# Hybrid attention layer on eight cores: 440 of the 128x128 transposes are issued as DMA transposes from SBUF to SBUF

## The chip, the cores and the metric

The kernel runs on all 8 cores of one Trainium2 chip. Each core computes one batch element of 4096 rows; the cores exchange nothing. The metric is the device time of the slowest core in microseconds (us).

## The reference

One decoder layer with two parallel branches, cut to what is computed:

```python
h = rms_norm(x, g_pre)
qa, ka, va, za, qb, kb, vb, zb, lr, gate_a, gate_b = split(h @ w_in)
# branch A: causal attention with two maps per head, ALiBi bias, 4 heads
p = softmax(qa @ ka.T * scale + bias)
oa = rms_norm((p[:, :, 0] - lam * p[:, :, 1]) @ va, g_sub_a) * (1.0 - lam_init)
ya = (oa * silu(za)) @ w_up_a
# branch B: gated linear attention (GLA) in chunks, 4 heads
glog = log_sigmoid(lr @ w_alpha + b_alpha) / 16
ob = rms_norm(gla_chunked(qb, kb, vb, glog), g_sub_b)
yb = (ob * silu(zb)) @ w_up_b
# merge
y = sigmoid(gate_a) * ya + sigmoid(gate_b) * yb
return x + rms_norm(y @ w_out, g_post)
```

## The kernel before

The 4096 rows are cut into 8 tiles of 512 rows (`t`), and a tile into 4 pieces of 128 rows (`s`). Stage `t` runs the attention of tile `t` (4 heads `h`, key blocks `kb` two at a time). Between the attention steps it runs a list of small units of matmuls, in this order: the merge and output of tile `t-1` (`u_e`, `u_f`, with the gate `u_za` of tile `t` ahead of the merge), the GLA projections of tile `t` (`gproj`: low rank, `vb`, `zb`, then `QB`/`KB`), and the Q, K, V projections of tile `t+1` (`u_qkv`) merged with the GLA recurrence of tile `t` (`core_units`). The preparation of the rows of tile `t+1` (`a_units`) is merged evenly into `gproj` by `merge`.

Each engine runs its instructions in the order in which the Python code emits them; waits on semaphores are worked out from the tiles that an instruction reads and writes. So an instruction that waits holds everything behind it on its engine. All DMAs are issued by SyncE (SP), in one such order: weights come from a scratch copy in DRAM to a ring of 7 pieces (L477), rows of x to three buffers `xb` (L318), results go out (L849).

The steps that the change touches:

- `a_stat` (L568) squares a row block of x on ScalarE (ACT) and uses `hb` as the place for the unused squares; `a_norm` (L580) writes the normalized rows to the same `hb` on VectorE (DVE). There are two `hb`, taken in turn, so `a_stat` of piece 2 has to wait until piece 0 is transposed, and piece 3 until piece 1 is.
- `a_tr` (L589) transposes the 8 blocks of `hb` on TensorE (PE) into a PSUM bank; DVE (L593) or ACT (L595) copies them to `hT`, from which all projections read. The first matmul of `u_qkv` reads all four pieces of `hT`.
- `g_tr` (L764) does so for the 4 heads of a gated GLA piece `gtB` (one buffer), copied by DVE (L766) to `gbT`; `p4` (L1029) for the 4 pieces of a gated attention head `gtA` (two buffers), copied by DVE (L1031) to `gaT`. The merge of the next stage reads `gaT` and `gbT`.
- `p1` to `p4` are the work after a head, kept in the list `posts`; `drain_posts` runs what is left of it.

Of the kernel before, what the change touches and what calls it, by code (L numbers as in the profile page):

```python
# [146 lines left out]
def _build(ntiles=NT):  # L147
    nc = bass.Bass("TRN2", target_bir_lowering=False)

    def din(name, shape, dt=F32):  # L150
        return nc.dram_tensor(name, shape, dt, kind="ExternalInput").ap()

    x = din("x", [S, D])
# [13 lines left out]
    out = nc.dram_tensor("out", [S, D], F32, kind="ExternalOutput").ap()  # L167
    wsc = nc.dram_tensor("wsc", [30, 128, PCOL], BF16).ap()

    P = _Prog()  # L170
    with ExitStack() as es:
        def SB(name, shape, dt):
            return es.enter_context(nc.sbuf_tensor("sb_" + name, shape, dt))

        def PSM(name, shape, dt):
# [8 lines left out]
        hb = [SB(f"hb{i}", [128, 1024], BF16) for i in range(2)]  # L184
        hT = [SB(f"hT{i}", [128, 8, T], BF16) for i in range(2)]
# [5 lines left out]
        gaT = [SB(f"gaT{i}", [128, 4, T], BF16) for i in range(2)]  # L191
        gtA = [SB(f"gtA{i}", [128, 4, 128], BF16) for i in range(2)]
        gtB = SB("gtB", [128, 4, 128], BF16)
        gbT = SB("gbT", [128, 4, T], BF16)
# [47 lines left out]
        poa = [PSM(f"oa{i}", [128, 512], F32) for i in range(3)]  # L242

        dma_names = (["stg%d" % i for i in range(8)] + ["wst%d" % i for i in range(NPIECE)] + ["wld%d" % i for i in range(NPIECE)]
                     + ["cstA", "cstB", "cstC"] + ["x%d" % i for i in range(7)] + ["st0", "st1", "st2"])
        sems = {}
        for nm in list(ENGS) + dma_names:
            sems[nm] = es.enter_context(nc.semaphore("s_" + nm))
# [328 lines left out]
        def a_norm(t, s):  # L577
# [3 lines left out]
                keys + [f"rstd{g}"], [f"hb{g % 2}"])  # L581
            x_load(sem)

        def a_tr(t, s):
            g = 4 * t + s
            b = falloc()
            v = bview(b)
            for kc in range(8):
                P.op("pe", lambda e, kc=kc: e.transpose(out=v[:, kc, :], in_=hb[g % 2][:, kc * 128:(kc + 1) * 128], identity=ident[:]),  # L589
                     reads=[f"hb{g % 2}", "ident"], writes=[b])  # L590
            h = hT[t % 2]
            if s % 2 == 0:
                dve(lambda e: e.tensor_copy(out=h[:, :, s * 128:(s + 1) * 128], in_=v), [b], [f"hT{t % 2}_{s}"])  # L593
            else:
                act(lambda e: e.activation(out=h[:, :, s * 128:(s + 1) * 128], in_=v, func=AF.Copy), [b], [f"hT{t % 2}_{s}"])  # L595
# [161 lines left out]
            pool(lambda e: e.tensor_tensor(out=gtB[:], in0=o, in1=szB[:, s, :].rearrange("p (h c) -> p h c", h=4), op=ALU.mult),  # L757
                 [f"s{4 + s % 2}", f"yT{s}"], ["gtB"])

        def g_tr(s):  # L760
            b = falloc()
            v = bview(b)
            for hd in range(4):
                P.op("pe", lambda e, hd=hd: e.transpose(out=v[:, hd, :], in_=gtB[:, hd, :], identity=ident[:]),  # L764
                     reads=["gtB", "ident"], writes=[b])
            dve(lambda e: e.tensor_copy(out=gbT[:, :, s * 128:(s + 1) * 128], in_=v[:, 0:4, :]), [b], [f"gbT{s}"])  # L766
# [124 lines left out]
        def merge(main, side):  # L891
            res = []
            n, m = len(main), len(side)
            j = 0
            for i, u in enumerate(main):
                res.append(u)
                while j < m and (j + 1) * n <= (i + 1) * m:
                    res.append(side[j])
                    j += 1
            return res + side[j:]  # L900

        def z(fn, *args):
            return (0.0, lambda: fn(*args), False)

        def w(c, fn, *args):
            return (c, lambda: fn(*args), False)

        def a_units(t):
            st = [z(a_stat, t, s) for s in range(4)]
            nm = [z(a_norm, t, s) for s in range(4)]  # L910
            tr = [w(0.6, a_tr, t, s) for s in range(4)]
            none = (0.0, lambda: None, False)
            return [st[0], st[1], nm[0], nm[1], none, tr[0], st[2], tr[1], st[3], nm[2], nm[3], none, tr[2], tr[3]]

        def core_units(k, gap, scrap):
            none = (gap, lambda: None, False)
            core = [z(g_decay, 0), w(0.6 * k, g_khat), none]
            for s in range(4):
                core += [w(0.3 * k, g_at, s)]
                core += [z(g_ew1, s - 1, scrap)] if s >= 1 else [none]  # L920
                core += [w(0.6 * k, g_o, s)]
                core += [z(g_ew2, s - 1)] if s >= 1 else []
                core += [w(0.3 * k, g_s, s), z(g_ew, s, scrap)]
                core += [z(g_decay, s + 1)] if s < 3 else []
                if s >= 1:
                    core += [none, w(0.4 * k, g_tr, s - 1)]
            return core + [none, z(g_ew1, 3, scrap), none, z(g_ew2, 3)]

        def stage_units(t):
            units = u_za(t)  # L930
            if t >= 1:
                head, body = u_e(t - 1)
                first = head + before(units, drain_posts)
                if t == 1:
                    first = merge(first, core_units(2.0, 0.5, False) + [z(lambda: None), z(lambda: None), w(0.4, g_tr, 3)])
                else:
                    first = first[0:8] + [w(0.4, g_tr, 3)] + first[8:]
                units = first + body + u_f(t - 1)
            u_lr, alpha, soft, decay, vbu, zbu, qku = u_glaproj(t)
            mid = [w(0.26, alpha(0)), w(0.26, alpha(1)), z(soft), z(decay)]  # L940
            gproj = u_lr + vbu[0:2] + mid[0:1] + vbu[2:4] + mid[1:3] + vbu[4:6] + mid[3:4] + vbu[6:] + zbu + qku
            if t >= 1 and t + 1 < ntiles:
                gproj = merge(gproj, a_units(t + 1))
            units = units + gproj
            if t + 1 == ntiles:
                units = units + core_units(3.0, 1.0, True)
            elif t >= 1:
                units = units + merge(u_qkv(t + 1), core_units(1.0, 0.0, True))
            return units
# [50 lines left out]
        def post_head(t, h):  # L1000
            gi = h % 2
# [21 lines left out]
                     ["oaf"] + [f"szA{a}" for a in range(4)], [f"gtA{gi}"])  # L1023

            def p4():
                b = falloc()
                v = bview(b)
                for a in range(4):
                    P.op("pe", lambda e, a=a: e.transpose(out=v[:, a, :], in_=gtA[gi][:, a, :], identity=ident[:]),  # L1029
                         reads=[f"gtA{gi}", "ident"], writes=[b])  # L1030
                dve(lambda e: e.tensor_copy(out=gaT[t % 2][:, h, :].rearrange("p (a q) -> p a q", a=4), in_=v[:, 0:4, :]),  # L1031
                    [b], [f"gaT{t % 2}_{h}"])
# [50 lines left out]
        for t in range(ntiles):  # L1083
# [13 lines left out]
            i = 0  # L1097
# [18 lines left out]
        emit_pv(*prev[0])  # L1116
        emit_pv(*prev[1])
        head, body = u_e(ntiles - 1)
        tail = head[0:4] + [w(0.4, g_tr, 3)] + head[4:] + body + u_f(ntiles - 1)
        for _, f, _ in tail:  # L1120
            f()
            run_post()
# [53 lines left out]
```

How the kernel before makes its waits and increments, by code:

```python
            def body(e):  # L127
                for o in my_ops:
                    waits = todo[id(o)]
                    on_ins = waits[-1:] if eng_name != "pe" else []
                    for s, v in waits[:len(waits) - len(on_ins)]:
                        e.wait_ge(sems[s], v)
                    ins = o.fn(e)
                    for s, v in on_ins:
                        if ins is None:
                            e.wait_ge(sems[s], v)
                        else:
                            ins.wait_op(sems[s], v, "sem-ge")
                    if o.needs_inc and ins is not None:
                        ins.then_inc(sems[o.sem], 16 if o.is_dma else 1)
```

## Time and profile before

| | us |
|---|---|
| median of 3 runs | 1598.61 |
| lowest and highest | 1595.65, 1601.07 |
| the profiled execution | 1599.34 |
| its span on the slowest core | 1597.8 |
| PE busy in the span | 1409.7 |
| ACT busy | 851.3 |
| DVE busy | 710.4 |
| POOL busy | 465.4 |

All times further on are from the profiled execution, counted from the start of its span on core 5. Rows are read from the page, from the timeline (start, duration, engine, line, operation, how many, and in brackets the idle time ahead and what ended it) and from the lists of what an engine waited for. In the timeline, equal instructions that follow each other are one row.

### The profile page before, as it was taken

What the parts mean: (1) busy time and instruction counts of PE and PEld (TensorE: products, weight loads), DVE (VectorE), ACT (ScalarE), POOL (GpSimd) and SP (SyncE); (2) the same over time, 40 slices, a digit from 0 to 9 for tenths busy, and PEclk for the clock granted to TensorE, in tenths of its full rate; (3) what the DMA queues carried; (4) which work ended last, traced back from release to release, by engine and by line L of the source; (5) the groups of instructions that cost most, each with busy time, mean ns of one, the idle gap of its engine ahead of it and who ended that gap; (6) DMA issues with size and microseconds to landing.
All of it is one profiled execution on the core that took longest, in us unless ns stands there. A gap on an engine that the chain in (4) does not pass through costs nothing.

```text
span 1597.8 us, 27753 instructions; the slowest of 8 cores (1585.8 to 1597.8 us)
## 1 busy us (share of the span) xinstructions
PE 1409.7 (88%) x10576; PEld 740.3 (46%) x10576; DVE 710.4 (44%) x1449; ACT 851.3 (53%) x1714; POOL 465.4 (29%) x469
## 2 busy tenths in 40 slices
PE   5877698699899988999789998899998999988888
PEld 2334344344455544555445554455554555544443
DVE  4557645552655344523545234453224541242434
ACT  4363345134544556355654665655668557667632
POOL 2035322343334321423214222043211340220441
PEclk9989899899999999999999999999999999999999
DMA  8868676533552336133541234522235322225023
GB/s 256 261 184 243 197 220 210 173 104 109 173 171 80 119 125 205 54 106 100 169 128 55 95 103 127 164 67 80 82 104 159 106 64 70 79 83 157 27 76 109
DMA packets 75437, 207.43 MB, mean 130 GB/s; under 512 B 7984, under 2 KB 26672, under 8 KB 75312
## 3 DMA queue, kind: packets, MB, share of 16 engines
q1 hardware_dynamic: 75312, 205.66, 41.6%
q8 instruction: 91, 1.49, 0.4%
q14 instruction: 34, 0.28, 0.1%
HBM read 173.12 MB, written 32.51 MB: 129 GB/s over the span
## 4 chain that ended last, share of the span: by engine, by line
PE 66%; DVE 12%; ACT 10%; DMA 5%; POOL 3%; issue 3%; SPq 0%; DVEq 0%; POOLq 0%; ACTq 0%
PE ps_q L270 32%; PE ps_f L270 20%; PE ps_oa L270 12%; ACT sb_PT L968 4%; DMA sb_KT<-w_in 2%; DVE sb_scr L846 2%; DMA wsc<-sb_wring 1%; ACT sb_junk L864 1%; ACT sb_ztmp L617 1%; DVE sb_scr L867 1%; DVE sb_rz L994 1%; DVE sb_wring L377 1%; DMA sb_xb<-x 1%; DVE sb_tmpo L996 1%; DVE sb_qtT L675 1%
## 5 line engine op out<-in xcount | busy, mean ns | idle before, releaser
L968 ACT ACTIVATE sb_PT<-ps_q 128x512 bf16<-128x512 f32 (+3 forms) x700 | 363.3, 566 | 235.4 <-PE ps_q L270 164.8
L270 PE MATMUL ps_oa<-sb_V,sb_PT 128*128 128x129 bf16 x4224 | 344.7, 221 | 15.9 <-ACT sb_PT L968 8.2
L270 PEld LDWEIGHTS ps_oa<-sb_V,sb_PT 128*128 128x128 bf16 x4224 | 285.1, 98 | 142.7 <-issue 35.7
L968 ACT ACTIVATE sb_PT<-ps_f 128x512 bf16<-128x512 f32 (+3 forms) x452 | 245.0, 566 | 166.5 <-PE ps_q L270 87.7
L270 PE MATMUL ps_q<-sb_hT,sb_wring 128*128 128x512 bf16 x1112 | 277.1, 385 | 12.0 <-ACT sb_hT L595 6.0
L813 POOL TENSOR_TENSOR sb_yT<-sb_scr 128x512 bf16<-128x512 f32 x64 | 81.2, 1269 | 391.5 <-DVE sb_scr L811 389.6
L270 PE MATMUL ps_f<-sb_hT,sb_wring 128*128 128x512 bf16 x680 | 168.8, 383 | 7.5 <-DVE sb_qtT L675 3.2
L270 PE MATMUL ps_q<-sb_QT,sb_KT 64*128 64x512 bf16 (+3 forms) x700 | 156.9, 365 | 17.2 <-DVE sb_yT L618 4.1
L270 PE MATMUL ps_q<-sb_wring,sb_hT 128*128 128x512 bf16 x584 | 153.2, 398 | 16.4 <-DVE sb_eblast L656 4.3
L270 PEld LDWEIGHTS ps_q<-sb_hT,sb_wring 128*128 128x128 bf16 x1112 | 100.3, 98 | 130.8 <-issue 42.3
L270 PE MATMUL ps_f<-sb_QT,sb_KT 64*128 64x512 bf16 (+3 forms) x452 | 127.2, 364 | 13.0 <-DVE sb_yT L618 2.6
L270 PE MATMUL ps_f<-sb_wring,sb_hT 128*128 128x512 bf16 x440 | 114.5, 392 | 9.8 <-DVE sb_eblast L656 4.0
L270 PEld LDWEIGHTS ps_f<-sb_hT,sb_wring 128*128 128x128 bf16 x680 | 61.1, 98 | 81.7 <-issue 26.8
L1006 POOL TENSOR_TENSOR sb_oaf<-sb_tmpo 128x512 f32<-128x512 f32 x32 | 40.7, 1271 | 199.7 <-DVE sb_tmpo L996 199.7
L807 DVE SCALAR_TENSOR_TENSOR sb_scr<-sb_scr,ps_q 128x512 f32<-128x512 f32 x39 | 26.8, 686 | 151.4 <-PE ps_q L270 151.4
L270 PEld LDWEIGHTS ps_q<-sb_wring,sb_hT 128*128 128x128 bf16 x584 | 54.5, 102 | 81.7 <-issue 39.2
L783 ACT ACTIVATE sb_scr<-ps_q 128x512 f32<-128x512 f32 x80 | 48.4, 606 | 58.9 <-PE ps_q L270 58.5
L270 PE MATMUL ps_q<-sb_wring,sb_yT 128*128 128x512 bf16 x280 | 69.2, 383 | 8.5 <-DVE sb_scr L867 6.0
L270 PEld LDWEIGHTS ps_f<-sb_wring,sb_hT 128*128 128x128 bf16 x440 | 39.6, 100 | 58.6 <-issue 26.4
L749 POOL TENSOR_TENSOR sb_rstdb<-sb_rsb,sb_lams 128x4 f32<-128x4 f32 x32 | 32.2, 1008 | 117.1 <-DVE sb_rsb L747 117.1
L373 ACT ACTIVATE sb_wring<-sb_KT,sb_smalls 128x256 bf16<-128x256 f32 (+1 forms) x72 | 35.4, 547 | 55.7 <-DVE sb_wring L377 31.9
L270 PE MATMUL ps_f<-sb_wring,sb_yT 128*128 128x512 bf16 x232 | 58.0, 381 | 5.0 <-DVE sb_scr L867 3.1
(171 smaller groups left out, 1831.4 us busy)
## 6 DMA issues: line engine op xcount, KB each, us to landing
sb_wring<-wsc SPq DMA_DIRECT2D x204, 512.0 KB, 3.6
sb_xb<-x SPq DMA_DIRECT2D x60, 512.0 KB, 5.6
sb_KT<-w_in SPq DMA_DIRECT2D x88, 256.0 KB, 7.5
out<-sb_scr SPq DMA_DIRECT2D x32, 512.0 KB, 3.5
wsc<-sb_wring SPq DMA_DIRECT2D x30, 512.0 KB, 7.5
sb_KT<-w_out SPq DMA_DIRECT2D x16, 256.0 KB, 7.1
sb_KT<-w_up_a SPq DMA_DIRECT2D x8, 256.0 KB, 7.4
sb_KT<-w_up_b SPq DMA_DIRECT2D x8, 256.0 KB, 7.9
```

What stands on the lines that cost most here:

```text
L270: P.op("pe", lambda e: e.matmul(out=out_, lhsT=lhsT, rhs=rhs, start=start, stop=stop, **kw), reads=reads, writes=writes)
L373: act(lambda e: e.activation(out=dst_ap, in_=src_ap, func=AF.Copy, scale=sc), rd, [key])
L377: dve(lambda e: e.tensor_scalar(out=dst_ap, in0=src_ap, scalar1=scale_ap, scalar2=scale_c, op0=ALU.mult, op1=ALU.mult), rd, [key])
L617: act(lambda e: e.activation(out=ztmp[:], in_=BANK[b][:, :], func=AF.Tanh, scale=0.5), [b], ["ztmp"])
L675: dve(lambda e, r=r, hh=hh: e.scalar_tensor_tensor(out=qtT[r, c, hh, :], in0=BANK[b][r, :], scalar=0.125, in1=eb[c][r, :], op0=ALU.mult, o ...
L749: pool(lambda e: e.tensor_tensor(out=rstdb[:, sl], in0=rsb[:, sl], in1=lams[:, 5:6].to_broadcast([128, 4]), op=ALU.pow), [f"rsb{s}", "nhal ...
L783: act(lambda e: e.activation(out=dst, in_=BANK[b][:, :], func=AF.Tanh, scale=0.5), [b], [key])
L807: dve(lambda e: e.scalar_tensor_tensor(out=ta[j], in0=ta[j], scalar=1.0, in1=BANK[b][:, :], op0=ALU.add, op1=ALU.mult), [b, f"s{j}"], [f"s ...
L813: pool(lambda e: e.tensor_tensor(out=yT[:, jj, :], in0=ta[j], in1=tb[j], op=ALU.add), [f"s{j}", f"s{2 + j}"], [f"yT{jj}"])
L846: dve(lambda e, hh=hh: e.scalar_tensor_tensor(out=zg[hh], in0=zg[hh], scalar=rstdz[:, g:g + 1], in1=ap[:, hh * 512:(hh + 1) * 512], op0=AL ...
L968: act(lambda e, pp=pp, m=m, c0=c0, b=b, cbias=cbias: e.activation(out=PT[pp][:, m, c0:512], in_=BANK[b][:, c0:512], func=AF.Exp, bias=cbia ...
L1006: pool(lambda e: e.tensor_tensor(out=oaf[:], in0=v4[:, :, 0, :], in1=v4[:, :, 1, :], op=ALU.add), ["tmpo0", "tmpo1", "tmpo2"], ["oaf"])
```

## The change

For tiles from 2 on, `a_tr` issues 8 DMA transposes from `hb` straight to `hT`. `g_tr` issues 4 from `gtB` to `gbT`, but for the last piece of the last tile. `p4` issues 4 from `gtA` to `gaT`, but for the last head of the last tile. All of them are issued by SP, in its one order. There are 192 + 124 + 124 = 440. The units that held PE transposes get no cost in the unit lists; `a_units` are merged into all of `gproj` but its last 8 units (`QB`/`KB`); and there is one more `drain_posts` four units into the gate units from tile 2 on.

```diff
+        def dma_tr(pairs, rkeys, wkey, sem):
+            for n, (dst, src) in enumerate(pairs):
+                P.op("sp", lambda e, dst=dst, src=src: e.dma_start(out=dst, in_=src, transpose=True), reads=rkeys,
+                     writes=[wkey] if n == 0 else [], dma=sem)
+            P.last_writer[wkey] = P.ops[-1]
         def a_tr(t, s):
             g = 4 * t + s
+            if t >= 2:
+                dma_tr([(hT[t % 2][:, kc, s * 128:(s + 1) * 128], hb[g % 2][:, kc * 128:(kc + 1) * 128]) for kc in range(8)],
+                       [f"hb{g % 2}"], f"hT{t % 2}_{s}", f"trx{g % 2}")
+                return
...
-        def g_tr(s):
+        def g_tr(s, on_pe=False):
+            if not on_pe:
+                dma_tr([(gbT[:, hd, s * 128:(s + 1) * 128], gtB[:, hd, :]) for hd in range(4)], ["gtB"], f"gbT{s}", "trb")
+                return
...
-            tr = [w(0.6, a_tr, t, s) for s in range(4)]
+            tr = [w(0.6 if t < 2 else 0.0, a_tr, t, s) for s in range(4)]
...
-                    core += [none, w(0.4 * k, g_tr, s - 1)]
+                    core += [none, z(g_tr, s - 1)]
...
-                    first = merge(first, core_units(2.0, 0.5, False) + [z(lambda: None), z(lambda: None), w(0.4, g_tr, 3)])
+                    first = merge(first, core_units(2.0, 0.5, False) + [z(lambda: None), z(g_tr, 3)])
                 else:
-                    first = first[0:8] + [w(0.4, g_tr, 3)] + first[8:]
+                    first = first[0:8] + [z(g_tr, 3)] + first[8:12] + [z(drain_posts)] + first[12:]
...
-                gproj = merge(gproj, a_units(t + 1))
+                gproj = merge(gproj[:-8], a_units(t + 1)) + gproj[-8:]
...
             def p4():
+                if h < 3 or t + 1 < ntiles:
+                    dma_tr([(gaT[t % 2][:, h, a * 128:(a + 1) * 128], gtA[gi][:, a, :]) for a in range(4)],
+                           [f"gtA{gi}"], f"gaT{t % 2}_{h}", f"tra{gi}")
+                    return
...
-        tail = head[0:4] + [w(0.4, g_tr, 3)] + head[4:] + body + u_f(ntiles - 1)
+        tail = head[0:4] + [w(0.4, g_tr, 3, True)] + head[4:] + body + u_f(ntiles - 1)
```

SP's order in stage 2, from the end of the output of tile 1 to the projections of tile 3, before (L318 loads x, L477 loads weights):

```order
L849 DMA out<-sb_scr 128x1024 [waits s_dve]
L318 DMA sb_xb<-x 128x1024
L477 DMA sb_wring<-wsc 128x2048 x4
L318 DMA sb_xb<-x 128x1024 [waits s_dve] x2
L477 DMA sb_wring<-wsc 128x2048 [waits s_pe] x4
L318 DMA sb_xb<-x 128x1024 [waits s_dve] x2
```

The same place now (L862 is the line of the output, L586 that of the DMA transposes):

```order
L862 DMA out<-sb_scr 128x1024 [waits s_dve]
L318 DMA sb_xb<-x 128x1024
L477 DMA sb_wring<-wsc 128x2048 x4
L586 DMA_TRANSPOSE sb_gaT<-sb_gtA 128x128 x4
L318 DMA sb_xb<-x 128x1024 [waits s_dve] x2
L586 DMA_TRANSPOSE sb_hT<-sb_hb 128x128 x16
L477 DMA sb_wring<-wsc 128x2048 [waits s_pe] x2
L318 DMA sb_xb<-x 128x1024 [waits s_dve] x2
L586 DMA_TRANSPOSE sb_hT<-sb_hb 128x128 x8
L477 DMA sb_wring<-wsc 128x2048 [waits s_pe] x2
L586 DMA_TRANSPOSE sb_hT<-sb_hb 128x128 x8
```

Sixteen transposes (pieces 0 and 1) stand between the two pairs of x loads, and pieces 2 and 3 stand on either side of a pair of weight loads.

ACT's order in stage 2 around `a_stat` of pieces 2 and 3, before (L568 is `a_stat`, L653 and L654 are exponentials of the GLA decay, L968 the exponentials of the attention, L617 the tanh of a gate, L595 a copy of transposed blocks):

```order
L568 ACTIVATE sb_hb,sb_ss<-sb_xb 128x1024 [waits s_x0,s_pe]
L968 ACTIVATE sb_PT<-ps_q 128x512 [waits s_pe] x2
L968 ACTIVATE sb_PT<-ps_f 128x512 [waits s_pe]
L968 ACTIVATE sb_PT<-ps_q 128x512 [waits s_pe]
L617 ACTIVATE sb_ztmp<-ps_f 128x512 [waits s_pe]
L617 ACTIVATE sb_ztmp<-ps_q 128x512 [waits s_dve,s_pe]
L595 ACTIVATE sb_hT<-ps_q 128x8x128 [waits s_pe]
L617 ACTIVATE sb_ztmp<-ps_f 128x512 [waits s_dve,s_pe]
L568 ACTIVATE sb_hb,sb_ss<-sb_xb 128x1024 [waits s_x1]
```

The same place now (L663 and L664 are the decay's exponentials, L981 those of the attention, L627 the tanh; `trx0` and `trx1` are the semaphores of the DMA transposes of pieces 0 and 1):

```order
L568 ACTIVATE sb_hb,sb_ss<-sb_xb 128x1024 [waits s_x0,s_trx0]
L663 ACTIVATE sb_scr<-sb_scr 128x512 [waits s_st0,s_dve]
L664 ACTIVATE sb_scr<-sb_scr 128x512 [waits s_act]
L663 ACTIVATE sb_scr<-sb_scr 128x512 [waits s_dve]
L664 ACTIVATE sb_scr<-sb_scr 128x512 [waits s_act]
L981 ACTIVATE sb_PT<-ps_f 128x512 [waits s_pe] x2
L981 ACTIVATE sb_PT<-ps_q 128x512 [waits s_pe] x2
L568 ACTIVATE sb_hb,sb_ss<-sb_xb 128x1024 [waits s_x1,s_trx1]
```

`a_stat` of pieces 2 and 3 now waits for DMA transposes where it waited for PE, piece 2 stands ahead of the decay, and the copy L595 is gone.

## Rows read from the trace of the kernel before

**Rows 1.** The page: busy time by engine, and the chain that ended last.

```profile
PE 1409.7 (88%) x10576; PEld 740.3 (46%) x10576; DVE 710.4 (44%) x1449; ACT 851.3 (53%) x1714; POOL 465.4 (29%) x469
...
PE 66%; DVE 12%; ACT 10%; DMA 5%; POOL 3%; issue 3%; SPq 0%; DVEq 0%; POOLq 0%; ACTq 0%
```

**Rows 2.** Timeline, PE, stage 6: two groups of transposes and what follows each.

```profile
1234.81 0.61 PE L589 MATMUL ps_q<-sb_ident,sb_hb 128*128 128x128 bf16 x8
1235.26 0.62 PE L270 MATMUL ps_oa<-sb_V,sb_PT 128*128 128x129 bf16 x8
...
1265.17 0.39 PE L1029 MATMUL ps_f<-sb_ident,sb_gtA 128*128 128x128 bf16 x4
1265.39 0.62 PE L270 MATMUL ps_oa<-sb_V,sb_PT 128*128 128x129 bf16 x8
```

**Rows 3.** What PE waited for, whole span: us in total, times, longest.

```profile
PE ps_f L1029 <- POOL sb_gtA L1022: 11.5, 4, 7.9
PE ps_q L270 <- ACT sb_hT L595: 6.3, 6, 1.3
PE ps_q L1029 <- POOL sb_gtA L1022: 4.2, 5, 1.7
```

**Rows 4.** SP's issues of DMAs in the timeline, and (last row) us from issue to landing.

```profile
1.50 0.42 SPq L283 DMA_DIRECT2D sb_ident<-ident  x1
3.85 7.74 SPq L364 DMA_DIRECT2D sb_KT<-w_in  x8
...
sb_ident<-ident SPq DMA_DIRECT2D x1, 32.0 KB, 3.1
```

**Rows 5.** Timeline of stage 1, where tile 2 is prepared.

```profile
281.31 0.90 SPq L318 DMA_DIRECT2D sb_xb<-x  x2
...
288.06 1.06 ACT L568 ACTIVATE sb_hb<-sb_xb 128x1024 bf16<-128x1024 f32 x1 [12.92 <-DMA sb_xb<-x]
...
291.22 1.01 PE L589 MATMUL ps_f<-sb_ident,sb_hb 128*128 128x128 bf16 x8 [9.42 <-DVE sb_hb L580]
...
292.43 0.75 DVE L580 TENSOR_SCALAR sb_hb<-sb_xb,sb_rstd 128x1024 bf16<-128x1024 f32 x1
...
302.61 1.89 PE L270 MATMUL ps_q<-sb_hT,sb_wring 128*128 128x512 bf16 x8 [1.21 <-ACT sb_hT L595]
```

**Rows 6.** Timeline of stage 2, where tile 3 is prepared.

```profile
431.41 0.69 DVE L665 CAST sb_vb<-ps_f 128x512 bf16<-128x512 f32 x1 [0.51 <-PE ps_f L270]
...
438.99 1.04 ACT L568 ACTIVATE sb_hb<-sb_xb 128x1024 bf16<-128x1024 f32 x1
...
461.60 1.90 PE L270 MATMUL ps_f<-sb_hT,sb_wring 128*128 128x512 bf16 x8
```

**Rows 7.** Timeline of stages 3 to 6: second copy of vb, first Q matmul.

```profile
601.76 0.68 DVE L665 CAST sb_vb<-ps_q 128x512 bf16<-128x512 f32 x1
...
638.45 3.49 PE L270 MATMUL ps_q<-sb_hT,sb_wring 128*128 128x512 bf16 x8 [1.25 <-ACT sb_hT L595]
...
793.01 0.69 DVE L665 CAST sb_vb<-ps_f 128x512 bf16<-128x512 f32 x1 [0.91 <-PE ps_f L270]
...
835.52 1.02 PE L270 MATMUL ps_q<-sb_hT,sb_wring 128*128 128x512 bf16 x4 [1.25 <-ACT sb_hT L595]
...
998.12 0.69 DVE L665 CAST sb_vb<-ps_f 128x512 bf16<-128x512 f32 x1 [1.41 <-PE ps_f L270]
...
1040.94 1.02 PE L270 MATMUL ps_q<-sb_hT,sb_wring 128*128 128x512 bf16 x4 [1.27 <-ACT sb_hT L595]
...
1216.28 0.69 DVE L665 CAST sb_vb<-ps_f 128x512 bf16<-128x512 f32 x1 [2.22 <-PE ps_f L270]
...
1257.79 1.02 PE L270 MATMUL ps_q<-sb_hT,sb_wring 128*128 128x512 bf16 x4 [1.07 <-ACT sb_hT L595]
```

More of the change, by code:

```diff
@@ L244, in _build @@
         dma_names = (["stg%d" % i for i in range(8)] + ["wst%d" % i for i in range(NPIECE)] + ["wld%d" % i for i in range(NPIECE)]
-                     + ["cstA", "cstB", "cstC"] + ["x%d" % i for i in range(7)] + ["st0", "st1", "st2"])
+                     + ["cstA", "cstB", "cstC"] + ["x%d" % i for i in range(7)] + ["st0", "st1", "st2", "trx0", "trx1", "tra0", "tra1", "trb"])
         sems = {}
```

## The prediction

> **What bounds the kernel now.** I read the page first: which engine is busy and which holds the chain. PE is busy 1409.7 of 1597.8 us and holds 66% of the chain that ended last; DVE holds 12% and ACT 10% [rows 1]. So PE's own work counts in full, and a wait on another engine counts only where PE ends up waiting for it. Then I read the timeline around the transposes, to price what leaves PE; then the list of PE's waits; then SP's issues, since SP takes the work over; and at last the stretch in which the next tile is prepared, stage by stage, because there a chain runs from x over ACT, DVE and PE to the Q projection. The sum is made against the profiled execution, 1599.3 us (span 1597.8 and 1.5 around it). That is 0.7 above the median of 1598.6, so no correction is needed.
>
> **What leaves PE.** A group of 8 transposes of x holds PE for 0.45 us (1234.81 to 1235.26), a group of 4 for 0.22 (1265.17 to 1265.39) [rows 2]. There are 24 groups of 8 (6 tiles) and 31 + 31 groups of 4: 10.8 + 13.6 = 24.4 us. PE also idles where it stands at these transposes or at their PSUM banks. For `gtA` that is 15.7 us in nine waits, of which one of 7.9 only moves to the merge that reads `gaT`, so 7.8 can go; copies of `hT` cost PE another 6.3, mostly one wait of about 1.2 at the first Q matmul of a stage [rows 3]. The remaining 62 small groups have smaller waits, and the copies of `gbT` and `gaT` free the banks later; I take 4 us for all of these. So the ceiling of the gain is about 24 + 8 + 6 + 4 = 42 us. ACT loses 12 copies and DVE 74, but neither is the bound, and I give that nothing. If the cover is gone there, it is a gain, not a loss.
>
> **What SP gets, and its price.** SP issues 440 more DMAs. The trace has no DMA transpose, so the time p that one holds SP is bounded by rows. The lower end is the issue of a plain 32 KB copy, 0.42 us; the first eight weight loads, which wait for nothing and write two pieces per partition, hold SP for 7.74 / 8 = 0.97 each; the upper end is a full trip of 32 KB from issue to landing, 3.1 us, if one had to end before the next starts [rows 4]. A transpose cuts 128 rows into 2-byte columns, so I place it by the load with many pieces and not by the plain copy: 1.14, which is also the geometric middle of the two ends. The landing after an issue I take as 3.1 throughout. In total SP would issue for 440 x 1.14 = 502 us of 1600, which it can spare; what matters is where the transposes stand in a chain.
>
> The Trainium skill gives a price in "VectorE: DVE Perf Modes", section "The three transpose paths": 1309 ns for a 128x128 bf16 transpose by DMA. No row here shows it; taken as p, the sum below would be about 30 us higher.
>
> **The chain in each stage.** `a_stat` of piece 2 writes `hb` of piece 0, so ACT now waits there for 8 DMA transposes, and at piece 3 for 8 more; behind it on ACT stand the attention's exponentials, without which PE soon runs out of work. Then `a_norm` of pieces 2 and 3, two x loads, and 16 more transposes must pass before the first Q matmul, which waits for all of `hT`. Let T0 be the time when SP has issued the x load behind `a_norm` of piece 1. Then:
>
> - piece 1 has landed at T0 + 15p + 3.1;
> - `a_stat` and `a_norm` of the last pieces take 288.06 to 293.18, 5.1 us [rows 5], and the two x loads 0.9, so 6.0;
> - piece 3 has landed another 15p + 3.1 later.
>
> Together T0 + 30p + 12.2, with p = 1.14 T0 + 46.4. The weight loads between wait for PE at places that PE reaches by then, so they add nothing.
>
> T0 in stage 1 is 281.31 + 0.90 = 282.2: SP is still busy with the first weights there, which is why ACT idles 12.9 us and PE 9.4 already [rows 5]. In the other stages `a_norm` of piece 1 now stands right behind the second copy of `vb` (it moved from unit 9 to 7), so T0 is that copy's start + 0.69 + 0.75 + 0.43. The first Q matmul then starts against before:
>
> - stage 1: 328.6 against 302.6, 26 later [rows 5];
> - stage 2: 433.3 + 46.4 = 479.7 against 461.6, 18 later; ACT alone would wait at piece 2 from 439 to T0 + 7p + 3.1 = 444.4 [rows 6];
> - stages 3 to 6: 650.0 against 638.5, 841.3 against 835.5, 1046.4 against 1040.9, 1264.6 against 1257.8, so 11.5, 5.8, 5.5 and 6.8 later [rows 7].
>
> That is 73.6 us. A stage whose Q matmul is set by this chain gets nothing from the 10.8 us of x transposes nor from the 6.3 at the copies of `hT`, so of the 42 only 42 - 17 = 25 remain. Net +48.6: 1599.3 + 48.6 = 1648 us. The slope is 6 x 30 = 180 us per us of p, so the change breaks even near p = 0.85.
>
> **The other waits.** `gtB` is one buffer: GpSimd's next write waits 3p + 3.1 = 6.5 us for the transposes ahead. The GLA units are spread over the projections, about four units of 1 to 2 us lie between, and PE reads nothing from GpSimd there in a hurry; nothing taken, at most 2 us of GpSimd wait for each of 21 pieces. `gaT` of the last head and the last `gbT` land about 7p + 3.1 = 11 us after they are issued, with eight gate units of PE work as cover; taken at nothing, at most 3 us a stage if that cover is short. Weight loads queue behind up to 16 transposes, 18 us, but the ring holds 7 pieces, so the next load is used several pieces later; nothing.
>
> **The rivals.**
>
> *A cheap issue (faster).* If a DMA transpose holds SP as a plain copy does, p = 0.42 to 0.7, the chain is T0 + 24.8 to 33.2. Only stage 1 is then late, by 4 us, and at p = 0.7 stage 2 by 5 and stage 1 by 13. With nearly the whole 42 us gained the time is 1599 + 4 - 42 = 1561, up to 1599 + 18 - 38 = 1579. For it speaks that most issues in the trace are near 0.4; against it that the loads with more pieces are not [rows 4]. The Trainium skill states a rule on this side: "Advanced Engine Details and Errata", section "X-Bar Transpose (TRN2)", says that transpose DMAs on TRN2 are as fast as regular ones. The trace has no row on it. It decides at p = 0.85.
>
> *One at a time (much slower).* If each transpose holds SP for p = 1.6 or more, the chain is T0 + 60, 14 us more in each of six stages: about 1648 + 83 = 1731 and up. Then SP is busy over 700 us with transposes and the weights come late as well. Against it: SP's slowest issue that waits for nothing is 0.97 [rows 4].
>
> *The chain is cut short (no change).* If landing takes 2 us and not 3.1, and p is near 0.9, the chain is T0 + 37: 18, 9, 2 and little else, 29 us, against a gain of 25 to 30. The time would be 1599.
>
> **How the numbers follow.** A measurement of this kernel can tell about 0.3% from no change. The forecast case (p from 0.95 to 1.5) has 0.55, the cheap issue 0.30, one at a time 0.07, no change 0.08. The forecast is 1648. The forecast case alone runs from 1614 to 1700. The range of 8 in 10 takes in most of the cheap issue and stops short of one at a time: 1565 to 1695. Faster by over 0.3%: 0.31; within 0.3%: 0.07; slower: 0.62.
>
> **What would show it.** In the trace after: the spacing of eight transposes on SP is p; ACT's idle ahead of `a_stat` of pieces 2 and 3, ended by a DMA into `hT`, and PE's idle ahead of the first Q matmul, are the chain, largest in stages 1 and 2. PE busy time should fall by about 24 us, and no PE wait for `gtA` should be left but the last. The forecast is wrong if eight transposes are issued in 4 us, if ACT does not wait at `a_stat`, or if PE finds other work through that wait.

## The result and the profile after

The changed kernel takes 1735.98 us (median; 1733.44 to 1744.16) where the kernel before takes 1598.61: a ratio of 1.0867, 95% interval 1.0844 to 1.0891. It is slower, as forecast, but by 137 us and not by 49, and the time lies outside the range that was given. One of its five executions, 1875.16 us at a lower clock on four of the eight cores, is left out of that span, and such executions are left out of every ratio below but not of the medians. The profiled execution took 1744.16 us, its span 1742.6 on core 2.

The page of the changed kernel, with the lines that answer to [rows 1]: busy time by engine, the clock granted to TensorE (PE) in 40 equal slices of the span, the chain that ended last by engine and by line, and the DMA packets:

```profile
PE 1414.2 (81%) x10136; PEld 724.9 (42%) x10136; DVE 676.0 (39%) x1375; ACT 840.8 (48%) x1702; POOL 468.5 (27%) x469
...
PEclk9988698699978998799987999979999899999999
...
PE 55%; SPq 16%; DVE 9%; DMA 8%; ACT 6%; POOL 3%; issue 3%; POOLq 0%; DVEq 0%; ACTq 0%
```

SP's issue queue had 0% of the chain in [rows 1] and has 16% now. PE has 440 instructions fewer and yet 4.5 us more busy time: its matmuls run slower. What the engines wait for (us in total, times, longest) says where:

```profile
ACT sb_hb L568 <- DMA sb_hT<-sb_hb: 107.9, 11, 32.2
POOL sb_gtB L767 <- DMA sb_gbT<-sb_gtB: 54.2, 19, 17.0
...
PE ps_q L270 <- DVE sb_vb L675: 44.9, 5, 24.4
PE ps_oa L270 <- ACT sb_PT L981: 27.4, 14, 10.3
...
PE ps_q L270 <- DMA sb_hT<-sb_hb: 24.6, 3, 9.9
...
PE ps_f L270 <- DMA sb_hT<-sb_hb: 21.6, 3, 8.3
...
PE ps_q L270 <- DMA sb_gbT<-sb_gtB: 17.7, 1, 17.7
```

ScalarE (ACT) waits 107.9 us at `a_stat` for transposes that still read `hb`. PE waits 46 us for `hT` itself, at the first Q matmul of each of six stages, and more for ACT and DVE, which stand behind that wait of ACT: in stage 1 ACT's longest wait (32.2 us) ends at 314.47, and PE's longest wait for DVE (24.4 us) ends at 318.33.

The timeline of stage 5 in the changed kernel shows the whole chain (start, duration, engine, line, operation, count, and in brackets the idle time ahead):

```profile
1105.53 0.61 PE L270 MATMUL ps_q<-sb_hT,sb_wlr 128*32 128x512 bf16 x8 [0.70 <-DVE sb_rsz L891]
1105.66 5.42 SPq L586 DMA_TRANSPOSE sb_gaT<-sb_gtA  x4
...
1116.54 3.78 SPq L586 DMA_TRANSPOSE sb_hT<-sb_hb  x3
...
1128.66 1.06 ACT L568 ACTIVATE sb_hb<-sb_xb 128x1024 bf16<-128x1024 f32 x1 [8.57 <-DMA sb_hT<-sb_hb]
...
1139.02 1.06 ACT L568 ACTIVATE sb_hb<-sb_xb 128x1024 bf16<-128x1024 f32 x1 [4.90 <-DMA sb_hT<-sb_hb]
...
1148.66 0.75 DVE L580 TENSOR_SCALAR sb_hb<-sb_xb,sb_rstd 128x1024 bf16<-128x1024 f32 x1
...
1169.48 2.51 SPq L586 DMA_TRANSPOSE sb_hT<-sb_hb  x2
```

The first transpose of x is issued 11.0 us behind the low-rank matmul that opens `gproj`, the last ends 55.5 us later (1171.99), and the first Q matmul (the row at 1173.24 further down) starts 56.7 us after the first transpose.

For each kernel I cut the span at three marks of the timeline: the low-rank matmul of a stage, the first eviction of Q in it (the DVE copy to `QT`), and the last eviction of V. The table gives the time to the low-rank matmul of stage 1, the sum over stages 1 to 6 from the low-rank matmul to Q, and the rest of the span. All are read from the profiled execution, on its slowest core. The first two rows are the result; the others are the experiments below.

| kernel | to stage 1's low-rank matmul | low-rank matmul to Q, six stages | rest | median |
|---|---|---|---|---|
| before | 250.9 | 316.3 | 1030.6 | 1598.6 |
| changed | 268.0 | 450.8 | 1023.8 | 1736.0 |
| x on TensorE | 272.0 | 315.2 | 1017.5 | 1606.5 |
| only x by DMA | 251.5 | 445.1 | 1035.7 | 1732.6 |
| only the order | 249.4 | 312.0 | 1034.9 | 1598.7 |
| one DMA per group | 251.7 | 336.3 | 1012.9 | 1601.4 |
| half of x | 268.8 | 354.0 | 1020.7 | 1645.5 |
| pairs | 265.2 | 356.8 | 1021.1 | 1645.6 |
| four buffers | 266.2 | 414.1 | 1022.0 | 1700.9 |
| one DMA, four buffers | 252.3 | 302.4 | 1011.2 | 1570.1 |
| the same, x only | 251.8 | 293.1 | 1034.1 | 1581.8 |
| the same, early | 253.3 | 340.7 | 1012.6 | 1608.5 |
| before, four buffers | 250.3 | 317.5 | 1029.9 | 1597.9 |
| two GLA buffers | 263.3 | 449.3 | 1017.1 | 1731.5 |

So of the 145 us between the two spans, 134.5 lie between the low-rank matmul and Q (35.2, 28.2, 23.4, 13.8, 16.9 and 17.0 in stages 1 to 6), 17.1 lie ahead of stage 1's low-rank matmul, and the rest gives 6.8 back.

### The profile page after: what moved, and what is told of

It reads as the page before. It is cut to its first block, busy times and chain, and to the rows that moved or that the text cites. A ratio compares the mean times of both kernels' runs of the same rounds, so it can differ in the third digit from the quotient of the medians.

```text
span 1742.6 us, 27212 instructions; the slowest of 8 cores (1716.4 to 1742.6 us)
## 1 busy us (share of the span) xinstructions
PE 1414.2 (81%) x10136; PEld 724.9 (42%) x10136; DVE 676.0 (39%) x1375; ACT 840.8 (48%) x1702; POOL 468.5 (27%) x469
## 4 chain that ended last, share of the span: by engine, by line
PE 55%; SPq 16%; DVE 9%; DMA 8%; ACT 6%; POOL 3%; issue 3%; POOLq 0%; DVEq 0%; ACTq 0%
PE ps_q L270 27%; PE ps_f L270 17%; SPq L586 14%; PE ps_oa L270 10%; DMA sb_KT<-w_in 2%; DMA sb_gbT<-sb_gtB 2%; ACT sb_PT L981 2%; DMA sb_hT<-sb_hb 2%; DMA wsc<-sb_wring 1%; DVE sb_scr L859 1%; ACT sb_junk L877 1%; DVE sb_scr L880 1%; POOL sb_gtB L767 1%; DVE sb_rz L1007 1%; ACT sb_ztmp L627 1%
## 5 line engine op out<-in xcount | busy, mean ns | idle before, releaser
L981 ACT ACTIVATE sb_PT<-ps_q 128x512 bf16<-128x512 f32 (+2 forms) x689 | 364.7, 568 | 228.9 <-PE ps_q L270 115.8
L981 ACT ACTIVATE sb_PT<-ps_f 128x512 bf16<-128x512 f32 (+3 forms) x463 | 253.8, 563 | 216.3 <-PE ps_q L270 128.2
L270 PE MATMUL ps_q<-sb_hT,sb_wring 128*128 128x512 bf16 x1152 | 293.0, 389 | 33.9 <-DMA sb_hT<-sb_hb 24.6
L270 PE MATMUL ps_q<-sb_wring,sb_hT 128*128 128x512 bf16 x664 | 186.5, 421 | 60.3 <-ACT sb_PT L981 19.7
L270 PE MATMUL ps_q<-sb_QT,sb_KT 64*128 64x512 bf16 (+2 forms) x689 | 163.5, 369 | 57.3 <-DVE sb_vb L675 28.8
L270 PEld LDWEIGHTS ps_q<-sb_wring,sb_hT 128*128 128x128 bf16 x664 | 64.2, 105 | 144.1 <-issue 98.6
L270 PE MATMUL ps_f<-sb_wring,sb_hT 128*128 128x512 bf16 x360 | 97.4, 405 | 7.5 <-ACT sb_PT L981 3.6
L568 ACT ACTIVATE sb_hb<-sb_xb 128x1024 bf16<-128x1024 f32 x28 | 29.7, 1060 | 137.2 <-DMA sb_hT<-sb_hb 107.9
L572 POOL TENSOR_TENSOR sb_rstd<-sb_rs,sb_lams 128x1 f32<-128x1 f32 x32 | 21.9, 683 | 225.5 <-DVE sb_rs L570 225.5
L270 PEld LDWEIGHTS ps_q<-sb_QT,sb_KT 64*128 64x128 bf16 x689 | 35.0, 94 | 85.7 <-issue 68.3
```

Of the source, the lines that this page charges most:

```text
L270: P.op("pe", lambda e: e.matmul(out=out_, lhsT=lhsT, rhs=rhs, start=start, stop=stop, **kw), reads=reads, writes=writes)
L568: act(lambda e: e.activation(out=hb[g % 2][:], in_=ap, func=AF.Square, accum_out=ss[:, g:g + 1]), keys, [f"hb{g % 2}", f"ss{g}"])
L572: pool(lambda e: e.tensor_tensor(out=rstd[:, g:g + 1], in0=rs[:, g:g + 1], in1=lams[:, 5:6], op=ALU.pow), [f"rs{g}", "nhalf"], [f"rstd{g}"])
L981: act(lambda e, pp=pp, m=m, c0=c0, b=b, cbias=cbias: e.activation(out=PT[pp][:, m, c0:512], in_=BANK[b][:, c0:512], func=AF.Exp, bias=cbia ...
```

## The experiments

All edits are to the changed kernel unless said otherwise. Times are medians; ratios are to the kernel before, with 95% intervals.

### Which part loses

**x back on TensorE**, and then the opposite, **only x by DMA**:

```diff
 # x back on TensorE
-            if t >= 2:
+            if t >= 99:
                 dma_tr([(hT[t % 2][:, kc, ...], hb[g % 2][:, ...]) for kc in range(8)], ...)
...
-            tr = [w(0.6 if t < 2 else 0.0, a_tr, t, s) for s in range(4)]
+            tr = [w(0.6, a_tr, t, s) for s in range(4)]
 # only x by DMA
-        def g_tr(s, on_pe=False):
+        def g_tr(s, on_pe=True):
...
-                if h < 3 or t + 1 < ntiles:
+                if False:
```

> The part of the change that concerns x is undone: rows of x are transposed by TensorE through PSUM in all tiles, at the places that the changed kernel gives them; the gated rows of the heads and of the GLA stay with the DMA. Theory 1, the loss is the serial chain of 32 transposes of x on SP in each of stages 1 to 6 (134 of the 145 us in the stretch from the low-rank matmul to the first Q eviction): that stretch falls back to 50 to 60 us per stage, and only the 17 us before the low-rank matmul of stage 1 stay: 1600 to 1625 us. Rival 1, the changed order of the units (the last eight units of the projections no longer have x beside them) is what delays Q: the stretch stays over 65 us in stages 3 to 6 and the time stays over 1660. Rival 2, the small packets of the gated rows hold up the weights: PE shows waits for weight pieces and the time stays over 1640.

> The other half: only rows of x (from tile 2) are transposed by the DMA; gated rows of the heads and of the GLA are back on TensorE. Theory 1, the x chain is the loss: the stretch from the low-rank matmul to the first Q eviction stays 65 to 85 us in stages 1 to 6; the 17 us wait ahead of the low-rank matmul in stage 1 goes, and so do the four transposes of gaT ahead of the first row group (5 us a stage), while TensorE has 248 transposes and their waits again (some 15 us): 1690 to 1725 us. Rival, the single buffer of the gated GLA rows and the transposes of the heads ahead of x set the loss: 1600 to 1650 us.

Measured: 1606.5 us (1.0058, 1.0040 to 1.0076) and 1732.6 (1.0842, 1.0815 to 1.0868). With x on TensorE the stretch to Q is back at 315.2; the 21 us ahead of stage 1's low-rank matmul remain, of which the rest gives 13 back, and the list of waits has the row for it:

```profile
PE ps_q L270 <- DMA sb_gbT<-sb_gtB: 19.0, 1, 19.0
```

With x alone on the DMA, the stretch stays at 445.1 and the wait ahead of stage 1 is gone (251.5). The x chain is the loss; the gated rows cost 17 to 21 us in one place. The second time is above the range expected, since the gated rows on TensorE add 12 us to the rest (1035.7), and the stretch is only 5.7 us shorter without `gaT` on SP.

**Only the order** of the changed kernel, every transpose on TensorE (both edits above together):

> The changed kernel with every transpose back on TensorE: only its changed order is left (the units of x beside all but the last eight units of the projections, the posts run out earlier in the next stage). Theory 1: the order is worth nothing by itself, 1592 to 1606 us. Rival 1: the order costs a part of the loss, 1615 us or more. Rival 2: the order is what gains in the run with one DMA per group and four buffers, 1585 us or less.

Measured: 1598.7 us (1.0001, 0.9990 to 1.0012). The order is worth nothing by itself, either way.

### What the price is of

**One DMA transpose per group**: 86 DMAs in place of 440, with the same blocks and bytes.

```diff
-                dma_tr([(hT[t % 2][:, kc, s*128:(s+1)*128], hb[g % 2][:, kc*128:(kc+1)*128]) for kc in range(8)],
+                dma_tr([(hT[t % 2][:, :, s*128:(s+1)*128], hb[g % 2][:])],
...
-                dma_tr([(gbT[:, hd, s*128:(s+1)*128], gtB[:, hd, :]) for hd in range(4)], ...
+                dma_tr([(gbT[:, :, s*128:(s+1)*128], gtB[:].rearrange("p h c -> p (h c)"))], ...
```

and the same for `gaT`.

> One edit to the changed kernel: each group of transposes (8 of a row group of x, 4 of a gated row group) becomes one DMA transpose of the whole [128, 1024] or [128, 512] row block, so 112 or so DMAs instead of 440, with the same bytes moved and the same 128x128 blocks. Theory 1, the price of 1.28 us that SP pays is one of the instruction: SP is held 4 x 1.28 = 5 us a stage for x instead of 41, the wait of TensorE for the rows of x at the start of Q falls back to that of the kernel before, and the stages keep what TensorE no longer transposes: 1575 to 1600 us. Theory 2, the price is one of the 128x128 block (about 10 us of SP for a group of x): the chain is as long as now and the time is 1720 to 1750 us. A price between the two per group, c, would show as about 6 x 4 x (10.2 - c) us less than 1736.

Measured: 1601.4 us (1.0024, 1.0006 to 1.0042), 135 us less than the changed kernel, where theory 1 said 136 to 161 less. SP's rows in the timeline, first two of the changed kernel with one block per DMA (from neighbouring windows that share one DMA), then of this one with eight:

```profile
490.87 10.02 SPq L586 DMA_TRANSPOSE sb_hT<-sb_hb  x8
499.65 11.44 SPq L586 DMA_TRANSPOSE sb_hT<-sb_hb  x9
```

```profile
302.36 1.24 SPq L586 DMA_TRANSPOSE sb_hT<-sb_hb  x1
...
645.75 1.24 SPq L586 DMA_TRANSPOSE sb_hT<-sb_hb  x1
```

One block holds SP for 10.02 / 8 to 11.44 / 9 = 1.25 to 1.27 us; eight blocks in one DMA can hold it for the same 1.24. So the price is of the instruction and not of the block. It is a least price, though: 8 of the 24 wide transposes of x show 1.24 and four 1.45 to 2.62, while the first two of each stage hold SP for 1.27 to 6.38, 45.7 us in twelve (more on them in the last section).

**Half of x** makes every second transpose and leaves the other blocks of `hT` with old values; **pairs** makes all of them, two blocks to a DMA. Both issue 16 a stage.

```diff
 # half of x
-    ... for kc in range(8)]
+    ... for kc in range(0, 8, 2)]
 # pairs
+    dma_tr([(hT[t % 2][:, 2*k2:2*k2+2, s*128:(s+1)*128], hb[g % 2][:, k2*256:(k2+1)*256]) for k2 in range(4)],
```

> Only every second of the eight transposes of each row group of x is made (the other four blocks of the transposed rows keep old values, so half of the x projections' inputs are left out of the transposing; every other instruction stays). The number of x transposes on SP in a stage falls from 32 to 16, by 20.5 us of SP per stage at the measured 1.28 us. Theory 1, a serial chain on SP that TensorE waits out: Q comes 18 to 20 us earlier in each of six stages until it meets the projections (in stages 3 to 6 these end about 15 us ahead of Q now, so part of it is lost): 90 to 115 us less, 1620 to 1646 us. Rival, the loss is TensorE's lower granted clock or DMA traffic in general and not the chain: less than 60 us less, over 1676 us.

> The changed kernel with x transposed two 128-column blocks at a time: four DMA transposes of [128, 256] for each row group of x, 16 a stage instead of 32, with all blocks moved (the run on half of x made 16 a stage too, but moved half of the blocks: 1645 us). Theory 1, SP pays by the instruction: 16 x about 1.25 us, so the time is that of the half of x, 1635 to 1660 us. Theory 2, a transfer of two blocks holds SP or the queue for longer than one: every 0.1 us more per instruction adds about 10 us, and a price by the block gives 1720 us or more.

Measured: 1645.5 us (1.0281, 1.0237 to 1.0325) and 1645.6 (1.0289, 1.0272 to 1.0307). Half the data or all of it, the time is the same, and the number of DMAs decides. The pairs kernel's row of SP and its time from issue to landing, and under it the landing in the changed kernel and with one DMA per group:

```profile
864.86 5.04 SPq L586 DMA_TRANSPOSE sb_hT<-sb_hb  x4
...
sb_hT<-sb_hb SPq DMA_TRANSPOSE x96, 3.8
```

```profile
sb_hT<-sb_hb SPq DMA_TRANSPOSE x192, 2.4
```

```profile
sb_gaT<-sb_gtA SPq DMA_TRANSPOSE x31, 4.4
sb_gbT<-sb_gtB SPq DMA_TRANSPOSE x31, 3.9
sb_hT<-sb_hb SPq DMA_TRANSPOSE x24, 6.2
```

Two blocks: 5.04 / 4 = 1.26 us of SP, and 3.8 to land; one block 2.4; four blocks 3.9 and 4.4; eight 6.2. So the width is paid in the landing, some 0.5 us a block on average from one block to eight, and here not on SP.

### What the reuse of the buffers costs

**Four buffers** for the rows of x; the two new ones take a part of `KT` that is free until tile 7 is written.

```diff
+        HB = ([(hb[i][:], [f"hb{i}"]) for i in range(2)]
+              + [(KT[:, 2*i:2*i+2, S-512:S], [f"hb{2+i}", f"stg{4*i+1}", f"stg{4*i+3}"]) for i in range(2)])
...
+            ap, keys = HB[g % 2 if g < 8 else g % 4]
```

> The changed kernel with four buffers for the normalised rows of x instead of two from tile 2 on (the two new ones lie in a part of KT that is free until tile 7 is written), so that ScalarE's sums of the third and fourth row group no longer wait for the transposes of the first and second; still 32 transposes of x a stage on SP. Theory 1, SP's serial time is the larger part and the reuse of the buffers the smaller: per stage the chain is first issue (about 16 us behind the low-rank matmul) + 32 x 1.28 = 41 us + 2.4 us landing = 59 to 62 us to the first Q eviction, where it is 72 to 73 now in stages 3 to 6: 10 to 15 us less in each of six stages, 1650 to 1675 us. Theory 2, ScalarE's waits (107.9 us in 11 waits) are the loss, through the exponentials behind them: nearly all of it returns, 1600 to 1630 us. Theory 3, the buffers cost nothing since SP is the bound throughout: 1720 us or more.

Measured: 1700.9 us (1.0612, 1.0563 to 1.0662), 35 less than the changed kernel, between theories 1 and 3. ACT's wait at `a_stat` for transposes is gone, and PE waits for `hT` instead, 104.5 us in six waits:

```profile
PE ps_q L270 <- DMA sb_hT<-sb_KT: 54.7, 3, 22.3
...
PE ps_f L270 <- DMA sb_hT<-sb_KT: 49.8, 3, 23.3
```

The first and the last row of the transposes in its stage 5:

```profile
1092.44 8.10 SPq L601 DMA_TRANSPOSE sb_hT<-sb_hb  x5
...
1129.66 10.02 SPq L601 DMA_TRANSPOSE sb_hT<-sb_KT  x8
```

They run from 1092.44 to 1139.68, 47.2 us for 32, where the two buffers need 55.5 (1116.54 to 1171.99 above). I had taken 41 for them and forgot the weight loads and x loads that stand between them on SP. A part of that gain is lost again, since the first one is issued 15.0 us behind the low-rank matmul and in the changed kernel 11.0. So SP's serial time is the larger part, and the buffers are worth some 6 us a stage.

**One DMA per group and four buffers** (groups three and four take two DMAs, since their buffers lie in two pieces):

> One DMA transpose per row group, with four buffers for the rows of x (groups three and four take two DMA transposes of 512 columns, since their buffers lie in two pieces): six x transposes a stage on SP, 7.4 us. With one DMA per group and two buffers, the stretch from the low-rank matmul to the first Q eviction was 65.0, 51.5, 51.3, 53.1, 55.5 and 59.9 us in stages 1 to 6, with ScalarE waits for the landing of 55 us in 6. Theory 1, what is left is the reuse of the buffers: the stretch falls to TensorE's own 45 to 50 us in stages 2 to 6 and to 45 to 55 in stage 1: 20 to 35 us less, 1566 to 1582 us. Rival, what is left is the landing of transposes behind weight loads in the DMA queues: 1595 us or more.

Measured: 1570.1 us (0.9791, 0.9737 to 0.9844). This beats both kernels; the runs of the kernel before beside it took 31 us more. The stretch to Q is 57.4, 44.0, 44.6, 46.5, 51.4 and 58.4 us; stages 1, 5 and 6 lie above what theory 1 said, though the time does not. Its page:

```profile
PE 1380.7 (88%) x10136; PEld 714.0 (46%) x10136; DVE 678.9 (43%) x1375; ACT 840.5 (54%) x1702; POOL 468.0 (30%) x469
...
PEclk9989799699999999999999999999999999999999
...
PE 69%; DVE 11%; ACT 8%; DMA 6%; issue 3%; SPq 1%; POOL 1%; DVEq 0%; POOLq 0%; ACTq 0%
```

With the same number of PE instructions as the changed kernel PE is busy 33.5 us less, the clock row has 7 or lower in two slices and not in six, and SP has left the chain.

**The kernel before with four buffers** is the control:

> The kernel before, all transposes on TensorE, with the four buffers for the rows of x. Theory 1: the buffers were no limit there, since TensorE's eight transposes of a group take about 1 us and free a buffer at once: 1592 to 1604 us, no change. Rival: the 31 us by which one DMA transpose per group with four buffers beat the kernel before come from the buffers, and 1580 us or less is measured here.

Measured: 1597.9 us (0.9996, 0.9986 to 1.0005). The buffers are worth nothing where TensorE transposes, and neither is the order (1598.7), so the gain of the 1570 us kernel comes from the DMA transposes. Order and buffers together, with TensorE transposing, were not run.

**Which of them gain**: the same kernel with the gated rows back on TensorE.

> One DMA transpose per row group of x with four buffers (1570 us with the heads and the GLA by the DMA too), and the gated rows of the heads and of the GLA back on TensorE. Theory 1: their 248 transposes cost TensorE 14 us and the waits for gated rows some 10, nearly all of it on the path: 1582 to 1594 us. Rival: these transposes were hidden beside other waits, and their place on SP ahead of x costs what they save: 1562 to 1574 us.

Measured: 1581.8 us (0.9903, 0.9886 to 0.9919). Rows of x give 16 us, and the gated rows 12 more (1581.8 to 1570.1; by the two ratios 18, with the wide interval of the 1570 us kernel). The table shows that by the DMA the gated rows lengthen the stretch to Q by 9 us (302.4 against 293.1) and shorten the rest by 23. That the 9 us come from `gaT`, which SP issues ahead of x, is likely but was not isolated.

**The units of x early**, merged into the first 12 units of `gproj`:

```diff
-                gproj = merge(gproj[:-8], a_units(t + 1)) + gproj[-8:]
+                gproj = merge(gproj[:12], a_units(t + 1)) + gproj[12:]
```

> As the run with one DMA transpose per group and four buffers, and the fourteen units that load, normalise and transpose x are spread over the first twelve units of the GLA projections instead of all but the last eight, so that the rows of x are ready while TensorE still has half of the projections ahead. Theory 1: Q then waits for TensorE alone, and the time is 0 to 10 us below that of the run before it, 1560 to 1580 us. Rival: the statistics on ScalarE wait for loads of x there and hold up the exponentials: 5 to 15 us above it.

Measured: 1608.5 us (1.0032, 0.9996 to 1.0068), 38 above the run with the same units later, more than either theory gave. ACT's waits at `a_stat` for loads of x, here and then in the 1570 us kernel:

```profile
ACT sb_KT L582 <- DMA sb_xb<-x: 42.7, 8, 23.8
...
ACT sb_hb L582 <- DMA sb_xb<-x: 36.8, 9, 8.1
```

```profile
ACT sb_hb L582 <- DMA sb_xb<-x: 26.7, 10, 5.4
...
ACT sb_KT L582 <- DMA sb_xb<-x: 19.7, 2, 18.7
```

79.5 us against 46.4: the sums stand ahead of the exponentials before their rows have come. That is the rival's mechanism; that it accounts for all 38 us was not shown.

### The one wait of the gated rows

**Two GLA buffers**: `gtB` gets a second buffer in the place of `junk`.

```diff
+        gtBj = [gtB[:], junk[:].rearrange("p (a b) -> p a b", a=4)]
...
-            pool(lambda e: e.tensor_tensor(out=gtB[:], in0=o, ...
+            pool(lambda e: e.tensor_tensor(out=gtBj[s % 2], in0=o, ...
```

> The changed kernel with two buffers for the gated GLA rows in place of one (the second takes the place of ScalarE's scratch for sums of squares), so that GpSimd writes the next rows while the DMA transposes the last. Theory 1: the 17 us wait of TensorE for gbT at the start of stage 1 comes from the GpSimd waits for that buffer (54 us in 19 waits, the longest 17.0) and goes; the six stages' stretches stay: 1712 to 1724 us. Rival, that wait is the order on SP (the transposes queue behind weight loads there) and not the buffer: 1732 us or more.

Measured: 1731.5 us (1.0807, 1.0749 to 1.0865), which can't be told from the changed kernel. PE's wait stays, at 23.5 us:

```profile
PE ps_q L272 <- DMA sb_gbT<-sb_junk: 23.5, 1, 23.5
```

My theory was wrong here. The timeline of the changed kernel, at the pieces of tile 0, shows GpSimd waiting 16.98 us for the buffer, but because SP issues the transposes that free it only after eight of `gaT` (11.1 us from 144.12) and staged weight loads, and then pays 4.9 us and more for each four:

```profile
162.47 4.95 SPq L586 DMA_TRANSPOSE sb_gbT<-sb_gtB  x4
171.09 1.15 POOL L767 TENSOR_TENSOR sb_gtB<-sb_scr,sb_yT 128x512 bf16<-128x512 f32 x1 [16.98 <-DMA sb_gbT<-sb_gtB]
...
189.31 5.70 SPq L586 DMA_TRANSPOSE sb_gbT<-sb_gtB  x4
...
197.44 1.86 PE L270 MATMUL ps_q<-sb_gbT,sb_wring 128*128 128x512 bf16 x4 [17.69 <-DMA sb_gbT<-sb_gtB]
```

With one DMA per group the time to stage 1's low-rank matmul is back at 251.7. So this wait, too, hangs on SP's price per instruction.

## Why the prediction was right or wrong

**The bound and the sign held.** PE held the chain, and what decided was the chain from x over ACT, DVE and SP to the first Q matmul, in every stage from 1 to 6, largest in stages 1 and 2. ACT waits at `a_stat` of pieces two and three, as said. The two runs at 16 DMAs a stage test the slope: at 0.63 us less per block it gives 113 us, and 90 were measured, part of it since the stretch to Q comes down to nearly its old length there (55 to 58 us in stages 3 to 5, 50 to 58 before). But that SP's time is priced by the DMA and not by the block was not in the text, and it is what matters most. The mechanism was right; what failed are sizes of its terms, terms that were put at nothing, and the gain. That 1736 lies where the rival with transposes one at a time put the time (1731 and up) is chance: that rival needs p of 1.6 or more.

**The price p was too low.** I took 1.14; it is 1.25 to 1.27. At 30 transposes in each of six stages, 0.13 us more are 23 us. The Trainium skill's 1309 ns ("VectorE: DVE Perf Modes", "The three transpose paths") agrees with the rows of SP for a single block, and was the better number. For a DMA of eight blocks the 1.24 us of SP show that it must not be multiplied by blocks. The other rule, that transpose DMAs are as fast as regular ones ("Advanced Engine Details and Errata", "X-Bar Transpose (TRN2)", in the Trainium skill), fails on SP, 1.25 against 0.42 us [rows 4], though in landing a block's 2.4 us are no longer than a plain copy's 3.1 [rows 4].

**The chain's fixed part was too short.** From the first transpose to the first Q matmul I had 46.4 us, 50.3 with p = 1.27; the timeline has 51.4, 50.9, 53.0, 55.4, 56.7 and 53.6, another 19 us in sum. Of these, 12 lie ahead of the first transpose of piece 2. The main step was the 6.0 us from `a_stat` to `a_norm` and the x loads, read from stage 1 of the kernel before [rows 5]: in stage 5 above, `a_norm` of the last piece starts 9.6 us after `a_stat`, since DVE works through units of a PE that is late. The other 7 lie between there and Q: "the weight loads between wait for PE at places that PE reaches by then, so they add nothing" was wrong, since a pair of them holds SP for 1.1 to 1.8 us between the last two pieces.

**The start T0** was off by +2.8, +3.9, +5.1, -3.0, -2.0 and +0.4 us in the six stages, 7 in all: four transposes of `gaT` stand ahead of x on SP (1105.66 above), which the text priced only for `gaT` itself.

Together 23 + 19 + 7 = 49. Counted from the low-rank matmul, the first Q matmul starts 123.5 us later in the six stages than before, which is 50 more than the 73.6 forecast, so these three terms account for it.

**The clock behind the wait was put at nothing.** The table counts up to the eviction of Q, and there 11 us more are lost: from the first Q matmul to its eviction it takes 26.2 us in six stages, and 15.2 before, with PE busy throughout and 99 matmuls where there were 100. The windows (us, busy time by engine, then granted clock, DMA share and GB/s) of stage 5 and the sum of six, of the kernel before and then of the changed kernel:

```profile
1040.94:1043.32 2.38, 2.38 (x20) 1.43 (x21) 0.00 (x1) 0.00 (x0) 1.44 (x2) 1.00 0.43 170
...
sum 15.18, PE 15.17 PEld 7.78 DVE 1.15 ACT 2.61 POOL 8.90; mean PE 2.53 PEld 1.30 DVE 0.19 ACT 0.43 POOL 1.48
```

```profile
1173.24:1178.79 5.55, 5.55 (x23) 2.31 (x24) 0.00 (x0) 2.07 (x4) 0.00 (x0) 0.50 0.57 192
...
sum 26.17, PE 26.16 PEld 10.95 DVE 0.01 ACT 4.13 POOL 0.00; mean PE 4.36 PEld 1.82 DVE 0.00 ACT 0.69 POOL 0.00
```

The changed kernel has 0.50 of the clock in five of the six windows and 0.56 in the sixth; the kernel before has 1.00 in five and 0.52 in one.

**The waits taken at nothing.** The wait for `gbT` at stage 1 costs 17.1 us. I gave up to 3 us a stage for it by looking at a stage's own cover of eight units, and did not follow SP's queue in stage 0, where staged loads fill it.

**The gain did not show.** Of the 25 net only 7 appeared outside the chain, so 18 are missing. Four of them go to the order, which alone has a rest of 1034.9 against 1030.6. Against that run the gated rows give 11 us in the rest, and 12 against the run with only x by DMA. With one DMA per group the rest is another 11 us shorter, so the single-block price eats a part of this gain too; through which wait was not traced.

The text also looked for 24 us less busy time on PE, and there are 4.5 more. The matmuls run slower, but between the low-rank matmul and Q, where PE waits for the chain anyway. The windows of that stretch in stage 5, of the kernel before and then of the changed kernel:

```profile
987.00:1043.00 56.00, 45.73 (x355) 24.99 (x355) 23.87 (x47) 36.31 (x68) 7.66 (x10) 0.94 0.53 170
```

```profile
1105.00:1179.00 74.00, 48.25 (x315) 24.18 (x316) 21.61 (x44) 34.66 (x66) 8.07 (x10) 0.79 0.48 144
```

40 matmuls fewer take 2.5 us more, at 0.79 of the clock against 0.94. From the eviction of Q to the next low-rank matmul both kernels have 0.99 or 1.00 in all six stages, so the clock can't be what took the 18 us. In sum, 48.6 forecast + 50 + 11 + 17 + 18 give the 145 us between the spans.

## What to carry to other kernels

Price a DMA transpose by the instruction on the queue that issues it, 1.25 us here, and give it the widest block that the layout allows; what width costs is landing time, which a spare buffer hides, and, in this kernel, time on the issuing queue at places where the DMA engines were full. When work moves to a queue that issues in order, write down everything that stands between the first and the last piece of the chain on that queue, and give the consumer's clock a term of its own. The same transposes were 137 us slower than TensorE or 31 us faster, by how many DMAs they took and how many buffers they had (1570.1 us, against the kernel before run beside it).

## What the runs showed of the hardware

The granted clock after a wait, in stage 5 of the changed kernel: four matmuls of one shape and tile pair just after a 6.14 us wait and 6.5 us later, and the window that follows (busy times, then the clock). The clock is 0.50 of full speed from 1173.24 to 1178.79 (shown above) and 1.00 from 1181 on, so both of its levels, 1.2 and 2.4 GHz, occur here:

```profile
1173.24 1.86 PE L270 MATMUL ps_q<-sb_hT,sb_wring 128*128 128x512 bf16 x4 [6.14 <-DMA sb_hT<-sb_hb]
...
1179.70 1.03 PE L270 MATMUL ps_f<-sb_hT,sb_wring 128*128 128x512 bf16 x4
```

```profile
1181.00:1190.00 9.00, 8.44 (x81) 4.84 (x77) 4.05 (x8) 4.13 (x8) 4.24 (x5) 1.00 0.26 75
```

The many small packets did no harm that I can find. The changed kernel moves far more of them:

```profile
DMA packets 145836, 221.86 MB, mean 127 GB/s; under 512 B 78384, under 2 KB 97072, under 8 KB 145712
```

The same row of the kernel before:

```profile
DMA packets 75437, 207.43 MB, mean 130 GB/s; under 512 B 7984, under 2 KB 26672, under 8 KB 75312
```

Still the weight loads land in 4.0 us against 3.6, and the half of x and the pairs, with 63024 and 75312 packets under 512 B, differ by nothing; one DMA per group still makes 67056 of them at 1601.4 us.

SP's price is not always 1.24 us for a wide transpose. With one DMA per group, the first two of x in each stage, whose rows are ready, hold SP for 7.43, 9.98, 8.29, 8.18, 4.37 and 7.72 us in stages 1 to 6. In stage 2 they stand behind four weight loads, a transpose of `gaT` and two loads of x:

```profile
444.12 9.98 SPq L586 DMA_TRANSPOSE sb_hT<-sb_hb  x2
...
622.11 8.29 SPq L586 DMA_TRANSPOSE sb_hT<-sb_hb  x2
```

The mean busy share of the DMA engines is 0.79 in the window of stage 1 and 1.01 to 1.04 in the others. But one of 1.24 us (302.36) has a share of 0.90, so a high share alone does not tell. A queue that is full would look so; no run here took those loads away, and it stays open.
